# Two prompt heads per mixing step, from probabilities scaled ahead of the turn, in a hybrid decoder step on one core

## What is computed

```python
def mla_prompt(...):                       # 6 heads, values of 64
    s = (einsum('bqhd,bkhd->bhqk', qn, k_nope) + einsum('bqhr,bkr->bhqk', qr, k_r)) * scale
    s = where(kpos <= qpos, s, NEG_INF)
    p = softmax(s, axis=-1)
    return einsum('bhqk,bkhd->bqhd', p, v)
...
# dilated_prompt: 6 heads of 64, softmax over keys t - j*dil in three patterns, combined by their sums
# xp = xp + concatenate([a_out, b_out, c_out], axis=-1) @ w_out
```

## Time and profile before

| | us |
|---|---|
| median of 3 runs | 2072.18 |
| lowest and highest | 2066.8, 2074.69 |
| span of the profiled execution | 2076.9 |
| TensorE busy in it | 2055.7 (99%) |
| VectorE, ScalarE busy | 1530.8 (74%), 1284.6 (62%) |
| the heads' loop, layer 0 | 91.7 to 187 |
| the turns of `oAB` to the output projection's start, layer 0 | 186.9 to 192.0 |

### The profile page before, as it was taken

The page is one execution under the profiler, slowest core; times in us unless marked ns, Lnnn a source line. Parts: engine busy times, 40 slices in busy tenths (PEclk is TensorE's granted clock), DMA queues, the critical chain, the costliest instruction groups (busy, mean ns, idle before and its releaser), DMA issues.

```text
span 2076.9 us, 40622 instructions
## 1 busy us (share of the span) xinstructions
PE 2055.7 (99%) x15546; PEld 1794.8 (86%) x15546; DVE 1530.8 (74%) x3491; ACT 1284.6 (62%) x2535; POOL 119.9 (6%) x138
## 2 busy tenths in 40 slices
PE   8999999999999999999999999999999999999998
PEld 6776799999999888788887758999999998887887
DVE  5844589868899776576678436998688997766766
ACT  5464445658888665565564544556688886555654
POOL 2200010000000010100022000100000001101000
PEclk9999999999999999999999999999999999999999
DMA  9443437776666888898763543577766668888886
GB/s 313 154 150 143 163 126 254 248 253 221 216 215 214 286 304 296 303 319 279 253 226 141 170 170 116 180 253 250 246 221 209 220 214 300 311 290 295 266 269 220
DMA packets 137376, 481.76 MB, mean 232 GB/s; under 512 B 25666, under 2 KB 42082, under 8 KB 130768
## 3 DMA queue, kind: packets, MB, share of 16 engines
q1 hardware_dynamic: 124640, 438.45, 62.6%
q0 software_dynamic: 10496, 40.42, 5.6%
q10 hardware_dynamic: 2048, 0.30, 0.1%
HBM read 475.83 MB, written 104.21 MB: 279 GB/s over the span
## 4 chain that ended last, share of the span: by engine, by line
PE 98%; DVE 1%; ACT 1%; DMA 0%; issue 0%; DVEq 0%; ACTq 0%
PE ps L1194 35%; PE ps L1241 33%; PE ps L827 4%; PE ps L875 4%; PE ps L919 3%; PE ps L1206 3%; PE ps L1157 2%; PE ps L927 2%; PE ps L1165 1%; PE ps L1161 1%; PE ps L884 1%; PE ps L1016 1%; PE ps L1180 1%; PE ps L1019 1%; PE ps L978 1%; PE ps L1032 1%
## 5 line engine op out<-in xcount | busy, mean ns | idle before, releaser
L2165 DVE TENSOR_TENSOR parts<-region,parts 128x1024 fp32r<-128x1024 f32 x512 | 625.6, 1222 | 300.6 <-ACT parts L1509 298.0
L1194 PE MATMUL ps<-tokens_hi,parts 128*128 128x256 f32 x4096 | 760.5, 284 | 0.0
L1509 ACT CAST parts<-region 128x1024 fp32r<-128x1024 f32 x512 | 538.8, 1052 | 271.0 <-PE ps L1241 221.2
L1241 PE MATMUL ps<-parts,parts_hw 128*128 128x512 f32 x3024 | 688.7, 389 | 0.0
L1241 PEld LDWEIGHTS ps<-parts,parts_hw 128*128 128x128 f32 x3024 | 566.8, 188 | 124.0 <-DVE parts_hw L2215 6.9
L1194 PEld LDWEIGHTS ps<-tokens_hi,parts 128*128 128x128 f32 x4096 | 636.6, 188 | 1.0 <-issue 0.8
L1194 PE MATMUL ps<-parts_hw,parts 128*128 128x256 f32 x2048 | 573.7, 280 | 0.0
L1194 PEld LDWEIGHTS ps<-parts_hw,parts 128*128 128x128 f32 x2048 | 386.5, 189 | 0.0
L1555 ACT ACTIVATE big<-ps 128x256 f32<-128x256 f32 (+31 forms) x252 | 131.7, 523 | 146.9 <-PE ps L1194 146.8
L1543 ACT CAST parts_hw<-big 128x256 fp32r<-128x256 f32 x256 | 170.9, 668 | 0.7 <-DVE big L2226 0.7
L1536 ACT ACTIVATE region<-region 128x128 f16<-128x128 f16 x512 | 169.2, 436 | 0.0
(11 more groups left out here) (316 smaller groups left out, 2172.9 us busy)
## 6 DMA issues: line engine op xcount, KB each, us to landing
region<-in_peer_uT SPq DMA_DIRECT2D x256, 512.0 KB, 4.1
region<-in_peer_v SPq DMA_DIRECT2D x256, 512.0 KB, 4.7
out<-in_state_win_k SPq DMA_DIRECT2D x112, 384.0 KB
out<-in_state_win_v SPq DMA_DIRECT2D x112, 384.0 KB
big<-in_window_keysT SPq DMA_DIRECT2D x16, 576.0 KB, 3.8
big<-in_state_win_v SPq DMA_DIRECT2D x48, 192.0 KB, 4.2
region<-in_w_out SPq DMA_DIRECT2D x4, 2048.0 KB, 8.2
big<-in_peer_wq SPq DMA_DIRECT2D x4, 2048.0 KB, 13.7
```

Source lines behind the costliest of these rows:

```text
L1194: mm = pe.matmul(ps[:, j % ZB, 0:SEQ], a, hp[b][:, c, :], start=(c == 0 and n == 0), stop=(c == KD - 1 and n == 2))
L1241: mm = pe.matmul(ps[:, 2 * half + t, :], w_t[a][:, 128 * t:128 * t + 128], v_t[b][:, 512 * half:512 * half + 512], start=(j == 0 and n == ...
L1509: act.copy(hi_t[n % HIGHS], rows_t[n % ROWS]).then_inc(high[l], 1)
L2165: dve.tensor_tensor(lo_t[n % ROWS], rows_t[n % ROWS], hi_t[n % HIGHS], ALU.subtract).then_inc(low[l], 1)
```

## The change

The division by the sums moves from the mixed values to the probabilities, ahead of their turn. VectorE takes the reciprocal and scales `prob` in place at the end of its step s, and a new semaphore `norm_ready` takes the place of `exp_ready` in front of TensorE's `turn_probs`. The mixing swaps operands: values are stationary (64 columns), turned probabilities move (256 columns for keys 0 to 127, 128 for keys 128 to 255), two heads at a time, the even head in PSUM partitions 0 to 63 and the odd one in 64 to 127, at steps 3, 5, 7, 9, 11 and 13, now ahead of `turn_probs` of that step. The result has heads by tokens, as the output projection wants it; VectorE copies it to `headT`, and the turns `mT`, their copies and `oAB` go. The job list has 12 jobs less, and the shift of the banks at the end is 2.

```diff
+        if s >= 2 and s % 2:
+            jobs.append((("O", s // 2 - 1), "V"))
         if 1 <= s <= 2 * NH:
             jobs.append((("PT", s - 1), "A"))
...
-        if s >= 2:
-            jobs.append((("O", s - 2), "V"))
...
-    jobs += [(("mT", g), "A") for g in range(2 * HP)]
...
-BANK = [LATE.get(name, (n if n < NUM["mT", 0] else n + 6) % 8) for n, (name, _) in enumerate(JOBS)]
+BANK = [LATE.get(name, (n if n < NUM["os",] else n + TAIL_BANKS) % 8) for n, (name, _) in enumerate(JOBS)]
...
                 def turn_probs(u):
-                    pe.wait_ge(exp_ready, u + 1)
+                    pe.wait_ge(norm_ready, u + 1)
...
-                def mix_values(u):
-                    wait_moved(pe, "PT", u)
-                    if u == 0:
+                def mix_values(g):
+                    wait_moved(pe, "PT", 2 * g + 1)
+                    if g == 0:
                         wait_moved(pe, "va", 1)
-                    o = begin("O", u)
-                    v = [va[:, t, 64 * u:64 * u + 64] if u < NH else z[:, t, VB + 64 * (u - NH):VB + 64 * (u - NH) + 64] for t in range(2)]
-                    pt = probT[:, u % 2, :]
-                    pe.matmul(o[:, 0:64], pt[:, 0:128], v[0], start=True, stop=True)
-                    pe.matmul(o[:, 64:128], pt[:, 128:256], v[0], start=True, stop=False)
-                    pe.matmul(o[:, 64:128], pt[:, 256:384], v[1], start=False, stop=True).then_inc(product[now[0]], 1)
+                    o = begin("O", g)
+                    for t in range(2):
+                        for u in (2 * g, 2 * g + 1):
+                            r0 = 64 * (u % 2)
+                            v = va[:, t, 64 * u:64 * u + 64] if u < NH else z[:, t, VB + 64 * (u - NH):VB + 64 * (u - NH) + 64]
+                            pt = probT[:, u % 2, 0:SEQ] if t == 0 else probT[:, u % 2, SEQ:384]
+                            mm = pe.matmul(o[r0:r0 + 64, 128 * t:SEQ], v, pt, start=(t == 0), stop=(t == 1), skip_group_check=True)
+                    mm.then_inc(product[now[0]], 1)
...
+                    if s >= 2 and s % 2:
+                        mix_values(s // 2 - 1)
                     if 1 <= s <= 2 * NH:
                         turn_probs(s - 1)
                     if s - 1 in PAST_STEP:
                         score_past(PAST_STEP.index(s - 1))
-                    if s >= 2:
-                        mix_values(s - 2)
...
-                wait_moved(pe, "O", 2 * NH - 1)
-                for g in range(2 * HP):
-                    turn("mT", g, parts=[(oAB[:, t, 128 * g:128 * g + 128], 128, 128, 128 * t) for t in range(2)])
                 wait_moved(pe, "olT")
...
-                for g in range(2 * HP):
-                    o = read("mT", g)
-                    act.copy(mixT[:, g, 0:SEQ], o[:, 0:SEQ]).then_inc(moved_a[now[0]], 1)
...
-                    u = s - 2
-                    if u >= 0:
-                        dve.wait_ge(exp_ready, u + 1)
-                        step(dve.reciprocal(rden[:, u, :], den[:, u, :]))
-                        o = read("O", u)
-                        settle()
-                        dve.tensor_tensor(oAB[:, :, 64 * u:64 * u + 64], o[:, 0:128].rearrange("p (t c) -> p t c", t=2),
-                                          rden[:, u, :].unsqueeze(2).to_broadcast([P, 2, 64]), ALU.mult).then_inc(moved_v[now[0]], 1)
+                    if s >= 2 and s % 2:
+                        g = s // 2 - 1
+                        o = read("O", g)
+                        dve.tensor_copy(headT[:, g, :], o[:, 0:SEQ]).then_inc(moved_v[now[0]], 1)
...
+                    if s < 2 * NH:
+                        dve.wait_ge(exp_ready, s + 1)
+                        step(dve.reciprocal(rden[:, s, :], den[:, s, :]))
+                        settle()
+                        for i, c0 in ((0, 0), (1, 128)):
+                            pr_ = prob[:, s % 2, c0:c0 + 128 * (i + 1)]
+                            e = dve.tensor_scalar(pr_, pr_, rden[:, s, i:i + 1], None, ALU.mult)
+                        e.then_inc(norm_ready, 1)
```

More of the change, by code:

```diff
@@ L149, in job_plan @@
     return jobs
+TAIL_BANKS = 2
 JOBS = job_plan()
@@ L303, in program @@
         va = cut(2 * 384).rearrange("p (t c) -> p t c", t=2)
-        oAB = cut(2 * 768).rearrange("p (t c) -> p t c", t=2)
+        headT = cut(2 * HP * SEQ).rearrange("p (g t) -> p g t", g=2 * HP)
         cut(2 * 286)
@@ L427, in program @@
         exp_ready = sem("exp_ready")
+        norm_ready = sem("probabilities_normed")
         y_ready = sem("conv_ready")
@@ L486, in program @@
         x_ld = [ctx.enter_context(nc.semaphore(f"x_loaded{t}")) for t in range(3)]
-        hsel_set = ctx.enter_context(nc.semaphore("head_selector_set"))
         ones_set = ctx.enter_context(nc.semaphore("ones_set"))
@@ L1131, in _ @@
                     turn("ycT", c, parts=tokens(yt, 128 * c))
-                wait_moved(pe, "mT", 5)
+                wait_moved(pe, "O", NH - 1)
                 wait_moved(pe, "os")
@@ L1138, in _ @@
                         t0, m = TOK[t]
-                        parts = [(mixT[:, k, t0:t0 + m], wview(5 + c)[:, k, :]) for k in range(KD)]
+                        parts = [((headT if t < 2 and k < 2 * HP else mixT)[:, k, t0:t0 + m], wview(5 + c)[:, k, :]) for k in range(KD)]
                         if t < 2:
@@ L1714, in _ @@
                     dve.wait_ge(ident_ld, 16)
-                    dve.tensor_reduce(hsel[:, 0:32], ident.rearrange("p (g h) -> p h g", g=4), AX, ALU.add).then_inc(hsel_set, 1)
+                    dve.tensor_reduce(hsel[:, 0:32], ident.rearrange("p (g h) -> p h g", g=4), AX, ALU.add)
                 input_low(0)
```

## The result

The changed kernel takes 2078.32 us (median of 20 runs, 2073.92 to 2082.03), the one before 2072.48 in as many runs beside them (2066.55 to 2075.47): ratio 1.0033, 95% interval 1.0023 to 1.0042. It is 5.8 us slower; the prediction was 7.3 us faster, with a range that ended at 2076. The sign was wrong and the time lies outside the range. That is within the 0.5% that the prediction called no change, but the interval over 20 runs of each leaves out zero. The profile of the changed kernel, from which all its rows come, is of the slowest of its 20 executions (2082.03 us, mean granted clock 0.992, where the others have 0.992 to 0.996).

The account below looks back on a forecast made before the run. TensorE, busy for 99% of the span, was taken as the bound. Saving 7.0 us a layer less 4.55 of waits left 4.9 in all; with 2.4 of clock, 7.3 us faster: 2065 us, range 2056 to 2076.

Parts of the forecast that it names:

- The mixes: Six new two-head mixes a layer on TensorE, 0.80 us each, replacing twelve old ones of 9.2 us a layer together.
- the 32-column rows: Old-trace matmuls in four column groups of 32 sharing all rows, which overlap; taken as nearest to the new mix.
- the serial case: Upper bound for a new mix on TensorE: no overlap of its matmuls, 2.1 us instead of 0.80.
- The waits that were forecast: TensorE waiting in the heads stage: 1.4 us in step 7, 0.4 in step 10, 2.15 in step 11, 0.3 for `os`.
- The other steps have cover.: In the heads stage's remaining steps, other TensorE work hides the scaling, so no further waits were counted.
- The 0.15 and 0.35 forecast for steps 2 and 4: Smallest waits: the turns of heads 1 and 3 come up 0.15 and 0.35 us short.
- The clock in mid-stage: Rival: the gap of 2.15 us in step 11 lets the clock fall, 2.5 us per layer, total 2070; chance 0.2.
- The clock at the end: Half clock at the stage's end and in the first projection half: 2.4 us back of 6.1 lost over both layers.
- the twelve turns that went: Turns of oAB at the stage's end, removed from TensorE: 2.55 us a layer on average counted as saved.
- The sum: Both layers: 4.9 us of work less waits plus 2.4 of clock, 7.3 us faster, giving 2065.
- The scaling hides: Rival: all waits in the heads stage but the last go, 4.25 us a layer, giving 2056.5; chance 0.13.
- The halves run one after the other: Rival: a mix's column halves run serially, 2.1 us a group, 15.6 us more, giving 2080.6; chance 0.12.

Follow-up runs that it names:

- e8: The changed kernel with both heads of a mix on the same 64 columns of TensorE, and two smaller copies instead of one: 2080.34 us, ratio 1.0034.
- e7: e4 with the new mix moved back behind the scores of the past and a third buffer for turned probabilities: 2062.62 us, ratio 0.995.
- e2: The changed kernel with VectorE scaling head 10 ahead of the convolution's statistics, in step 10 alone: 2073.05 us, ratio 1.0004.
- e3: The changed kernel with unread matmuls filling the two long gaps, 7 in step 7 and 8 in step 11: 2074.71 us, ratio 1.0015.
- e10: The kernel before with only the division moved ahead of the turn of the probabilities, old mixes and end turns kept: 2087.38 us, ratio 1.0069.
- e4: The changed kernel with ScalarE's exponentials ahead of copying the turned past and VectorE scaling right behind its taps: 2067.26 us, ratio 0.9979.
- e1: The changed kernel with PSUM banks numbered as if the six missing mixing jobs were still there: 2077.83 us, ratio 1.0027.
- e6: The changed kernel without reciprocals or scaling, the turns waiting for the exponentials as before: 2073.85 us, ratio 1.0006.
- e12: The changed kernel with the mixes behind the scores of the past and three buffers, both queues as in the change: 2081.69 us, ratio 1.004.

## Why the prediction was wrong

Its steps, in its order.

- **The mixes.** 0.80 us was forecast and 0.80 measured, in all rows at full clock. The reading of the 32-column rows as the nearest to the unknown operation was right, and e8 shows what the serial case costs (1.44, not the 2.1 of the upper bound, which was priced by full-width scores). The rule of the Trainium skill that spoke against it ("TensorE: Matmul & The Clock Gate", packing small matmuls: loads overlap only across different row groups) is not borne out here: in e7 loads of this mix (L998) start at 130.14 and 130.35 us while, by the profile (in which ends of matmuls are modelled), earlier matmuls of it on the same rows still run. And it speaks of loads alone; that the streams would queue as well was the prediction's own step. The page "TensorEngine Tiling (Array Packing)", key properties, lets tiles load and multiply in parallel, 128x64 among them, and the trace agrees: in e7 the two first matmuls start at 129.87 and 129.88 us.
- **The waits that were forecast.** Right in place and size: forecast 1.4 for step 7 (measured 1.63), 0.4 for step 10 (0.35), 2.15 for step 11 (1.92), 0.3 for `os` (0.30). Following one event through three queues, each against the old run, came within a quarter of a microsecond in these four.
- **"The other steps have cover."** This step failed. The prediction asked for each turn whether VectorE is ready, and gave the old mixes a price of 0.84 us each, all of it saved. It didn't ask what ran in ScalarE during those 0.84 us. In steps 2, 3 and 9 it was the copy that frees the bank of the next job, and 0.17 + 0.85 + 0.85 us came back as waiting; e7 puts the cover back and the two of 0.85 go. The 0.15 and 0.35 forecast for steps 2 and 4 did not show at all, and the 0.78 us that TensorE lost at the start of step 10 before is gone, which the prediction had not counted either. On balance the waits are 6.07 - 0.99 = 5.1 us a layer against 4.55: in the sum this error is only 1.1 us for both layers. For what could be had it is the larger one, as e7 shows.
- **The clock in mid-stage.** This step failed too, and it is the largest error. It stood as a rival at 0.2, for one gap and 2.5 us a layer, and the forecast put it at nothing. In the profiled execution it fell behind both long gaps, in both layers: 3.2 us a layer by the rows, 6.4 in all. e2 (gap gone, fall gone), e3 (gap filled, no fall) and e10 (longer gap, longer fall) show by three ways that the gap is the cause. The argument against it, the nines of the clock row over gaps of a few tenths, said nothing of gaps of 1.6 and 1.9 us: the old trace held no such gap in the stage, so it was no evidence.
- **The clock at the end.** Forecast: 2.4 us back. Measured: half clock from 189.4 to 196.2 us in layer 0 and from 1220.2 to 1227.0 in layer 1, and the first projection half at 15.48 and 15.69 us against 15.97 and 15.43: 0.2 us back. The clock returns 3.1 and 3.5 us after the projection's start, before 4.0 and 2.8. The term counted a gain twice: the twelve turns that went had run at half clock themselves (2.70 us for 12, where 20 take 2.33 at full), so what a shorter weak stretch gives was already in their 2.55 us.
- **The sum.** Split by the estimate over all executions, in work at full clock and in clock. At full clock the twelve turns are 1.4 us a layer and not 2.55, so of the forecast's 7.3 us, 2.6 were work less waits and 4.7 were clock. Measured: +0.3 and +5.7. The first part is off by 2.9 us: 1.1 by the balance of the waits, 1.8 open. e7, where nearly all waits are gone, says the same: 11.6 us less at full clock, 1.0 of them by fewer waits, so the work saved is 5.3 us a layer, where the prediction's 7.0 make 5.85 at full clock. One candidate, not tested, is that old mixes beside waiting cost less than their 0.84. The second part is off by 10.4: the profiled pair shows 6.4 lost in mid-stage, and at the end 1.7 given back instead of 4.7 (13.7 us of half clock against 17.1).
- **The rivals.** "The scaling hides" is what e4 built by hand, and it gave 2067, not 2056.5, as the first copies still had to be waited for; with those covered as well (e7) the time was 2062.6. "The halves run one after the other" was wrong, and its price was twice too high (1.3 us a mix forecast, 0.64 in e8).

## What to carry to other kernels

Before work is taken from an engine that is busy all the time, ask of each removed piece what ran on the other engines during it: the piece may have been the cover of a copy, and then only the part that exceeds that copy is saved. In the profiled execution each of the waits of 1.63 and 1.92 us on a saturated TensorE was paid nearly twice, once in itself and once in the clock behind it; in e1 the same wait in two pieces, 0.85 and 0.59, was not. And where the clock differs from one execution to the next, look at the mean granted clock of each before a profile is compared with a median. Lastly, a change that lengthens a way between engines should move its new step to the front of each queue that it passes: with exponentials and scaling first and the mix where the old one was, the same idea that lost 5.8 us gained 9.9.

## What the runs showed of the hardware

The profiles of the changed kernel, e1, e2, e6, e8, e10 and e12 have 18 idle stretches of TensorE of 1.6 to 2.7 us in the stage, amid turns and short matmuls. In or within 1.4 us behind 15 of them the granted clock fell from 2.4 to 1.2 GHz, and the length of the half clock was not the same: 3.4 us in the changed kernel, 6.8 behind the gaps of 2.23 and 2.72 in e10 and e12. The three without a fall are the 1.92 us of e1 in layer 1, the 1.63 of e6 in layer 1 and the 2.04 of e12 in layer 0; the same gap in the other layer had one. So the length of a gap alone doesn't decide. No wait of 1.28 us or less did it in mid-stage. In e8, with mixes of 1.44 instead of 0.80 us, the fall at the end was half as long and the mean clock the highest of all (0.9968); that the fall in step 11 was gone there may as well be due to its shorter gap. And the clock differs between executions of one program, from 0.992 to 0.996 in the changed kernel. I had thought of the clock as a matter of long stretches with nothing to do, and of one end of the stage; here it made the difference between a change that comes out even and one that loses.
